# Prompt attention in a hybrid decoder step: the residual addition ahead of the mask operation of the same step on VectorE

## What is computed

```python
def block(args):                       # 128 queries at a time
    qb, iqb, iwb, pos = args
    idx, valid = _indexer_topk(iqb, iwb, ik, pos, topk)      # 256 keys per query
    return _sparse_attend(qb, _gather_rows(k, idx), _gather_rows(v, idx), valid)

logits = jnp.einsum('btgrd,btkgd->btgrk', qg, k_sel)
logits = jnp.where(valid[:, :, None, None, :], logits, -jnp.inf)
p = jax.nn.softmax(logits, axis=-1)
o = jnp.einsum('btgrk,btkgd->btgrd', p, v_sel)

y_p = y_p + (o * jax.nn.silu(gate)) @ w_out                  # the residual addition
```

## Time and profile before

| | before |
|---|---|
| median of 3 executions | 1778.81 us |
| lowest and highest | 1774.89 and 1779.67 us |
| the profiled execution, first to last instruction | 1776.7 us |
| PE busy | 1689.8 us, 95% |
| DVE busy | 1262.0 us, 71% |
| mean granted TensorE clock | 0.976 of full speed |

### The profile page before, as it was taken

One profiled execution on the slowest core, in us unless ns is written; L12 is line 12 of the kernel. 1 busy time (PEld: TensorE's weight loads), 2 busy tenths in 40 slices (PEclk: granted clock), 3 DMA queues, 4 the chain that ended last, 5 costly groups with the idle time before them and its releaser, 6 DMA issues. The chain is left out here.

```text
span 1776.7 us, 26877 instructions
## 1 busy us (share of the span) xinstructions
PE 1689.8 (95%) x10109; PEld 967.8 (54%) x10109; DVE 1262.0 (71%) x2081; ACT 764.5 (43%) x1812; POOL 533.1 (30%) x632
## 2 busy tenths in 40 slices
PE   8999999999998999998999999999998879999999
PEld 6534434444446566665444544444435866777775
DVE  2399969999996798992696554646454677777773
ACT  2357867874225343333211242232212656554551
POOL 2502200100112111000225777777722512222320
PEclk9999999999999999999999999999998869999999
DMA  7406440110026111202413455555689444434321
GB/s 231 136 1 220 160 146 15 40 49 30 30 79 253 65 48 58 98 24 80 127 44 101 128 172 172 168 171 166 198 283 338 126 150 102 130 100 109 94 58 59
DMA packets 164024, 211.35 MB, mean 119 GB/s; under 512 B 45576, under 2 KB 114720, under 8 KB 163872
## 3 DMA queue, kind: packets, MB, share of 16 engines
q1 hardware_dynamic: 121912, 153.62, 26.6%
q0 software_dynamic: 16896, 50.35, 9.2%
q10 hardware_dynamic: 25088, 5.66, 1.5%
HBM read 165.86 MB, written 43.74 MB: 118 GB/s over the span
## 5 line engine op out<-in xcount | busy, mean ns | idle before, releaser
L1578 POOL DMA_INDIRECT scores<-in_cache_k,rowidx x128 | 135.6, 1059 | 39.5 <-issue 36.7
L2211 POOL DMA_INDIRECT home<-in_cache_v,rowidx x128 | 132.9, 1038 | 39.0 <-issue 38.4
L1189 DVE MAX8 top_v<-scores 128x8 f32<-128x4100 f32 x32 | 141.6, 4427 | 0.4
L1191 DVE FIND_INDEX8 top_i<-top_v,scores 128x8 uint32<-128x4100 f32 x32 | 141.5, 4422 | 0.0
L1193 DVE MATCH_REPLACE8 scores<-top_v,scores 128x4100 f32<-128x4100 f32 x32 | 141.2, 4413 | 0.0
L186 ACT ACTIVATE junk_topk_h<-key_mask,bs_cand 128x640 f32<-128x640 f32 (+1 forms) x104 | 102.0, 983 | 32.0 <-DVE bs_cand L196 25.8
L1399 PE MATMUL ring<-w_out_att,ogT_blk 128*128 128x512 f32 x256 | 113.0, 600 | 1.0 <-ACT ogT_blk L1432 0.9
L965 PE MATMUL acc<-w_out_att,xnT 128*128 128x512 f32 x256 | 112.7, 593 | 0.0
L965 PE MATMUL acc<-w_kvq,xnT 128*128 128x512 f32 x256 | 111.4, 593 | 0.0
L3600 PE MATMUL PY<-home,ogT_dn 128*128 128x512 f32 x224 | 101.8, 596 | 0.0
L1432 ACT COPY pT_blk<-tp_blk 128x512 f32<-128x512 f32 (+3 forms) x96 | 43.2, 486 | 121.4 <-PE tp_blk L1369 121.2
(11 more groups left out here) (560 smaller groups left out, 3598.4 us busy)
## 6 DMA issues: line engine op xcount, KB each, us to landing
S_s<-in_dn_w_in SPq DMA_DIRECT2D x24, 512.0 KB, 4.8
qkv_d<-y_ch SPq DMA_DIRECT2D x24, 512.0 KB, 3.7
qkv_t<-qkv_d SPq DMA_DIRECT2D x8, 1536.0 KB, 8.0
home<-in_dn_w_in SPq DMA_DIRECT2D x5, 2048.0 KB, 13.9
x<-in_x_all SPq DMA_DIRECT2D x8, 512.0 KB, 3.5
w_kvq<-in_att_w_in SPq DMA_DIRECT2D x2, 2048.0 KB, 13.0
qT_d<-qTb SPq DMA_DIRECT2D x8, 512.0 KB, 2.7
gate_d<-sgate SPq DMA_DIRECT2D x8, 512.0 KB, 3.1
```

Source lines behind the costliest of these rows:

```text
L1189: link(dve.max(v, scores[:]))
L1191: dve.max_index(top_i[:, 8 * r:8 * r + 8], v, scores[:])
L1578: pool.indirect_dma_start(rows[:, j % KR, c, :], None, ck, bass.IndirectOffsetOnAxis(ap=idx[:, c, query(j):query(j) + 1], axis=0)).then_in ...
L2211: pool.indirect_dma_start(vg[:, j % VR, c, :], None, cv, bass.IndirectOffsetOnAxis(ap=rowidx[:, c, query(j):query(j) + 1], axis=0)).then_i ...
```

## The change

In `prompt_attend`, in DVE's loop over the steps, the residual addition is put ahead of the mask operation that is issued in the same step:

```diff
             for hc in range(NH):
                 i, h = divmod(hc, H)
+                if i >= 1 and h == RES_AT:
+                    residual(i - 1)
                 if hc + 2 < NH:
                     masked(hc + 2)
-                if i >= 1 and h == RES_AT:
-                    residual(i - 1)
                 if hc - 2 >= 4 * LAST_HALF:
                     normed(hc - 2)
```

## The result

| | before | changed |
|---|---|---|
| median | 1774.89 us (7 executions) | 1765.97 us (7 executions) |
| lowest and highest | 1772.36 and 1783.64 us | 1762.98 and 1773.82 us |
| ratio, 95% interval | | 0.9944 [0.9923, 0.9965] |
| the profiled execution, first to last instruction | 1776.7 us | 1765.7 us |

The change is faster by 8.9 us between the medians. The three executions of before that were known beforehand, with their median of 1778.81, are three of its seven, which have 1774.89.

A forecast was written before the change was run, and what follows sets the result against it. PE was taken to bound the kernel, waiting six times for the residual addition. Gains of 1.40, 1.20, 0.91, 0.77, 0.51 and 1.07 sum to 5.86 us, other terms zero: 1778.81 - 5.86, or 1772.9 us, range 1769.5 to 1777.5.

The forecast's parts named there:

- The cause and the places: Ends of blocks 1 to 6: PE waits for the residual addition, queued behind head 7's mask operation; six waits, 5.5 us.
- the rule of the Trainium skill: Highest occupancy bounds a kernel; by that block 6 is DVE's and the swap gains nothing; the forecast took 1.07 us.
- So each wait is worth its figure and 0.16: Blocks 1 to 6: idle time plus 0.16 us of lost overlap per wait, together 6.46 us at most.
- The mask operation: Head 7's, moved back by up to 1.2 us; PE has 0.7 us of room at the least; cost zero.
- The last block: Block 7: only the loss, mask operation and exponential later; cost zero, by 0.6 us; 1.15 at most.
- PE needs them at 809.71: End of block 7: ACT's copies end at about 809.1, 0.6 us before PE needs them.
- Rival 1: DVE is the bound and keeps the gain from block 3 on: 1776.2 to 1778.8 us; chance 0.12.
- Rival 2: Blocks 1 to 7: the mask operation becomes the late one, cost 8.5 us, 1787.3 us; chance 0.03.
- 1778.81 - 5.86: Whole kernel: median of three runs of before less the gain in blocks 1 to 6, 1772.9 us.
- I take zero: Behind the stage: no net effect of the granted clock; run spread of 1774.89 to 1779.67 us taken as its scatter.
- The sign that the text gave: From block 0's first logits to the stage's last matmul, 5.9 us less in the profile after.
- rival 3: The clock in the scan falls otherwise, about 5 us more or less: 1768 to 1778 us; chance 0.09.

The follow-up runs named there:

- the early extraction: On top of the change, extraction instructions from block 2's projection to block 6's issued one place earlier: 1770.24 us, 0.9983 against before; repeat 0.9966.
- The dose: Head 7's mask operation done twice in blocks 1 to 7, here added to the changed kernel: 1770.89 us, 0.9983 against before.
- the 183: All executions of the unchanged kernel of before taken together: mean 1775.34 us.
- the dose in the order of before: Head 7's mask operation done twice in blocks 1 to 7, added to the unchanged kernel: 1778.99 us, 1.0029 against before.

## Why the prediction was right in its mechanism and wrong in its time

- **The cause and the places: right.** The residual addition starts 0.13 us behind y in block 1, five waits of PE are gone, and one is left. It was said to be about 0.6 us; the row shows 0.44, and with the overlap of 0.16 that is 0.60. Blocks 4 and 6 gained 0.81 and 1.07, though DVE is busy there for 92 and 97% of the earlier trace rows. By the rule of the Trainium skill, page "Perfetto Trace Analysis", section "Identifying the Most-Contended Engine", that I set beside it, block 6 is DVE's. That it therefore gains nothing was my reading of the rule, and the runs contradict it.
- **The worth of a wait: low by 0.07 us in five blocks.** The step "So each wait is worth its figure and 0.16" counts the idle time ahead of the logits only, and 6.46 wasn't the most that these waits hold: the early extraction took 6.94. The group of logits behind a wait is also longer itself: 0.88 us in the earlier trace rows and 0.81 now, 1.10 and 1.02, 1.32 and 1.25, 1.53 and 1.46, 1.74 and 1.67. Block 6 still waits, its row stays at 1.96, and its 1.07 was exact. In block 4 part of it is spent again, since there was no margin (0.81 instead of 0.84). The sum is 6.19 instead of 5.86.
- **The mask operation: right. The last block: right in its figure, and nearly not.** The stretch that begins in block 7 cost nothing. The step "PE needs them at 809.71" named the wrong reader, though. Its 0.6 us of room is there for the products (0.61), but the transposes ahead of them have 0.08. Of the 1.13 us that the exponential came later, PE had room for 1.21.
- **Rival 1 (DVE keeps the gain): refuted.** Its mark, growing waits of PE for `nmx_blk`, didn't come: 0.9 us as before. Blocks 3 to 6 keep 3.43 us by themselves.
- **Rival 2 (the mask operation late): refuted, with 0.08 us to spare at the end of block 7.** The dose shows that its path is real beyond that.
- **The failed step is the sum, "1778.81 - 5.86", with its range.** The text took the median of three executions as the level of before and gave the scatter of two medians "some 2.5 us". Seven executions put that level at 1774.89, the 183 at 1775.3, with single ones from 1765.7 to 1786.4. Of the 6.9 us between 1772.9 and 1765.97, the level accounts for 1778.81 - 1774.89 = 3.9 and the gain for 8.9 - 5.9 = 3.1 (rounded). The level alone would have put the forecast at 1774.89 - 5.86 = 1769.0, below its own range. Of the 3.1, 0.33 is the mis-sized wait, and 1.5 went away with more executions (8.9 to 7.4). From the level of the 183, the stretches' 6.19 would give 1769.2.
- **"I take zero" for the clock behind the stage: not what the profiles show.** They have 1.1 to 3.6 us less there in each profile of the changed order. The sign that the text gave, from the first logits of block 0 to the last matmul of the stage 5.9 us less, came out at 7.8 us in the first pair of profiles (296.3 to 288.6) and at 8.7 to 8.8 in the repeats, since it takes in the last projection with its 1.70 us and the stage's start with its 0.9. It was named as a possibility of either sign, in the scan (rival 3); it came closer, right behind the stage. How much of it lasts to the end, and whether it belongs to the change, isn't settled.

## What to carry to other kernels

Where a slot of a ring is freed by a short operation, put the operation ahead of whatever else its engine could do then, if the slot is the next one wanted; look for the other operation's own room first, against every waiter and not only its data's reader (here the one that wanted an emptied tile had 0.08 us, the reader 0.61). Measure such an edit from one fixed instruction to the next around each wait, which repeated here to 0.02 us, and let the timings say only whether it arrives. State the forecast as a ratio, and don't hang an effect of 0.3% on a median of three.

## What the runs showed of the hardware

**An operation of DVE three times as long beside one of POOL.** At the end of block 7, L1498, a SCALAR_TENSOR_TENSOR of 128 columns, takes 1.02 us in the kernel without the edit in block 7, while POOL's L1331 runs:

```profile
802.04 1.04 POOL L1331 TENSOR_TENSOR w_kvq<-w_kvq,ri_blk 128x512 f32<-128x512 f32 x1 [3.26 <-DVE ri_blk L1488]
802.21 1.02 DVE L1498 SCALAR_TENSOR_TENSOR w_kvq<-w_kvq,ri_blk 128x128 f32<-128x128 f32 x1 [0.26 <-ACT w_kvq L1445]
```

With the edit in block 7 alone it stands behind L1331, and takes 0.35:

```profile
807.43 1.04 POOL L1331 TENSOR_TENSOR w_kvq<-w_kvq,ri_blk 128x512 f32<-128x512 f32 x1 [3.25 <-DVE ri_blk L1488]
808.72 0.35 DVE L1498 SCALAR_TENSOR_TENSOR w_kvq<-w_kvq,ri_blk 128x128 f32<-128x128 f32 x1 [1.39 <-ACT w_kvq L1445]
```

ACT's two copies (L1432, 1.07 us) run beside it both times, so they aren't the cause. The operation reads two tiles from SBUF, the memory that the engines share. The Trainium skill, page "GPSIMD Engine Reference", section "Specifications", says that GpSimd shares its SBUF interfaces with VectorE and contends with its instructions of two SBUF inputs; these rows agree, with 0.67 us for one such operation. No instruction is listed as waiting for L1498 in either profile, and the last stretch is as long in both, so it cost nothing here.

**Stretches at half clock.** A profile of this program has 58 to 102 us in which TensorE is granted half its speed, and differs in this from the next profile of the same kernel: 76 to 89 us in the four of before, 58 to 83 in the four of the changed kernel. Right behind the attention four of four profiles of before have one inside the last projection and none of the five of the changed order, but two kernels with the order of before and a dose have none there either.

**What such a stretch costs differs from place to place.** The same 3.4 us at half clock cost 1.70 us inside the last projection, 1.29 behind a wait for the residual addition (the dose in the order of before), and some 0.1 in the next stage, ahead of a wait for a DMA.
